# Loading an expert's gate, up and down weights as one transfer of 12 KB rows, and another order of the first attention output products

## The chip, the cores and the metric

The kernel runs on one core of one Trainium2 chip. The metric is the device time of one launch in microseconds (us), the median of several runs. The kernel before took 1279.79 us (three runs, 1278.62 to 1281.28).

## What is computed

One inference step of a one-layer streaming encoder, for 1024 prompt tokens, 128 sample tokens (8 streams of 16) and 16 meta tokens, width 1024, all in 32-bit floats. After an input projection, a pooling branch and a sparse attention (8 heads, 2 key and value heads), the two branches are merged, and a mixture of experts follows:

```
x1 = x + W_out( sig(g_A) * Pool(h) + sig(g_B) * (Attn(h) @ w_attn_out) ),   h = RMSNorm(x)
h2 = RMSNorm(x1);  each of 1152 tokens picks one group of 8 experts and 2 experts in it
out = x1 + sum over its 2 experts of  weight * ( silu(h2 @ w_gate[e]) * (h2 @ w_up[e]) ) @ w_down[e]
```

There are 32 experts. Gate and up are 1024 x 128 each and down is 128 x 1024: 512 KB each, 1.5 MB an expert. The last step is a final RMSNorm.

## The kernel before

Each engine runs its own program, written out by hand in `build`, and they meet at semaphores. SP issues nearly all plain transfers, on one queue, in program order; POOL issues the indirect ones (gathers and scatters) on another.

**Attention output** (PE from line 1198, evacuation by DVE from line 2086). For each of 8 columns of output features `c`, PE computes three products, one for each 384 tokens (`TOK3`), from the attention result in two parts (`o_hi`, `o_lo_p` or `o_lo_s`) and the weights in two parts (`wao_hi`, `wao_lo`). Product `u = 3c + j` goes to bank `u % 4`, and from `u = 4` PE waits for the evacuation of `u - 3` (`b6_evac`). DVE multiplies by the gate (`sB`, loaded by SP at line 807) and adds the pooling part. PE waits once, at line 1198, until all 24 attention groups have been written out by DVE (`a_oe`, lines 2028 and 2029). The groups run over blocks of 128 tokens from the last to the first, so the last group written is that of tokens 0 to 127. SP waits for the same at line 814, and then loads weights, gates, `w_out` (4 MB in rows of 4 KB, line 824) and x. ACT splits each column's weights (line 1650) and POOL forms their rest (line 2498).

**Output projection, routing** (PE from line 1284). Nine tiles of 128 tokens. SP stores the normalized rows to `h2_d` (line 866), and the first expert weights are loaded between those stores: experts 0 to 3 whole, the down weights of expert 6 early (line 864), experts 4 and 5, and gate and up of expert 6 last (line 872).

**Experts** (PE from line 1380). `list_d` holds each expert's tokens; an expert takes up to 128 rows. Weights live in seven slots (`eslot`, 12 KB in each of 128 partitions: gate, up, down). For expert `e` PE runs `gate_up_split(e)` (lines 1361, 1362, 1365), transposes the gathered rows of `e + 1` (line 1333), multiplies expert `e - 1`'s activations by its down weights (line 1346), and turns the activations (line 1371). ACT copies the high parts of gate and up of expert `e + 2` (`expert_upper`, lines 1786 and 1787), after waiting for all three pieces:

```
act.wait_ge(ew_in[e % NSLOT], 48 * (e // NSLOT + 1))
```

The gate and up product of `e` waits for these parts. ACT also scales half of the down product (line 1801), DVE the other half (line 2239). POOL then scatters the rows of expert `e - 1` to `y_d` (line 2525) and, in program order before the next scatter, issues the gather for expert `e + 3` into one of three buffers (line 2520). Gathers skip places past the end of a list, and so do scatters.

SP's loop at line 884 refills the slots: gate and up of `e + 7` as two transfers once `gate_up_split(e)` is done (`gu_done`, lines 842 and 843), the down weights of `e + 7` once expert `e`'s down product is done (`dn_done`, line 847), which comes after gate and up of `e + 8` in the queue. The three arrays `wg`, `wu` and `wd` lie apart in DRAM, and each transfer has 128 rows of 4 KB. An expert with more than 128 tokens is finished by a loop at line 2552, which loads weights into slot 0 again.

**End** (from line 895): SP loads the experts' rows back (line 900, two neighbouring rows at a time, 8 KB in one piece), PE and DVE add them, and the result is normalized and stored.

## Time and profile before

| | |
|---|---|
| median of 3 runs | 1279.79 us (1278.62 to 1281.28) |
| the profiled execution | 1279.34 us, its span in the profile 1277.5 us |
| PE busy | 1227.9 us, 96% of the span |
| PE weight loads | 1068.0 us, 84% |
| DVE, ACT, POOL busy | 917.7, 511.9 and 440.8 us |
| mean granted TensorE clock | 0.989 of full speed |
| moved by transfers | 163.84 MB in 79457 packets |
| chain that ended last | PE 84%, DMA 6%, POOL 3%, ACT 3%, DVE 2% |

The profile is one execution of the program. Times are from the start of the span. "PE" is TensorE, "PEld" its weight loads, "SPq" SP's queue of instructions. A name such as L847 is a line of the kernel. In a timeline, "x4" counts merged instructions, and brackets hold the idle time of the engine before the first of them and what ended it. "Share" in a table of stretches is the mean busy share of the core's 16 transfer engines.

### The profile page before, as it was taken

The page shows a single profiled execution, that of the slowest core. Times are in us where ns is not written, and L with a number is a line of the kernel's source. Part 1 is how long each engine was busy: PE and PEld are TensorE (multiplying, and loading weights), DVE is VectorE, ACT ScalarE, POOL GpSimd, SP SyncE. Part 2 cuts the span into 40 slices and gives each one's busy share as a digit, 9 for nine tenths or more (in the row PEclk, how much of TensorE's full clock was granted, in tenths as well). Part 3 has the DMA queues.
Part 4 walks back from the last instruction along what each step waited for, and adds up shares of the span by engine and source line. Part 5 has one row for each costly group of instructions (what it writes and reads, how often), then busy time and mean ns, then how long its engine had stood idle before and what let it go on. Part 6 is the DMA issues. An engine that isn't in the chain of part 4 may idle for free.

```text
span 1277.5 us, 21420 instructions
## 1 busy us (share of the span) xinstructions
PE 1227.9 (96%) x7577; PEld 1068.0 (84%) x7577; DVE 917.7 (72%) x2179; ACT 511.9 (40%) x1117; POOL 440.8 (35%) x740
## 2 busy tenths in 40 slices
PE   6999999999999999998999999999999979999987
PEld 6999999999999999998777766999788858887753
DVE  5667888889998999874677776232666668877747
ACT  6554323232321112224666554000432247766634
POOL 5803565676873115654000010210011233433310
PEclk9999999999999999998999999999999989999998
DMA  7201322222223221103000231944321469999749
GB/s 274 72 28 56 99 65 79 42 79 42 71 56 121 90 70 53 34 1 104 2 1 17 63 95 58 324 136 162 116 83 47 153 227 334 364 336 348 291 172 366
DMA packets 79457, 163.84 MB, mean 128 GB/s; under 512 B 12418, under 2 KB 48082, under 8 KB 78210
## 3 DMA queue, kind: packets, MB, share of 16 engines
q1 hardware_dynamic: 64977, 128.84, 29.6%
q0 software_dynamic: 12656, 27.62, 6.5%
q10 hardware_dynamic: 1728, 6.10, 1.2%
q8 instruction: 61, 1.00, 0.3%
q14 instruction: 35, 0.28, 0.1%
HBM read 137.86 MB, written 39.21 MB: 139 GB/s over the span
## 4 chain that ended last, share of the span: by engine, by line
PE 84%; DMA 6%; POOL 3%; ACT 3%; DVE 2%; SPq 1%; issue 1%; POOLq 0%; ACTq 0%; DVEq 0%
PE bank L921 12%; PE bank L920 12%; PE bank L922 12%; PE bank L1133 5%; PE bank L1115 3%; PE bank L1214 3%; PE bank L1208 3%; PE bank L1346 2%; PE bank L1051 2%; PE bank L1225 2%; PE bank L1226 2%; PE bank L1227 2%; DMA region_t<-ffn_input_scratch,small_i 2%; DMA region_h<-in_wd 2%; PE bank L1210 2%; PE bank L1361 1%
## 5 line engine op out<-in xcount | busy, mean ns | idle before, releaser
L1961 DVE MAX8 small<-region_kv 128x8 f32<-128x272 f32 (+4 forms) x241 | 190.2, 828 | 47.6 <-DVE region_kv L1966 47.5
L920 PE MATMUL bank<-h_hi,w_hi 128*128 128x384 f32 (+1 forms) x576 | 196.1, 340 | 0.0
L921 PE MATMUL bank<-h_lo,w_hi 128*128 128x384 f32 (+1 forms) x576 | 196.1, 340 | 0.0
L1966 DVE MATCH_REPLACE8 region_kv<-small,region_kv 128x272 f32<-128x272 f32 (+4 forms) x241 | 195.5, 818 | 0.0
L922 PE MATMUL bank<-h_hi,w_lo 128*128 128x384 f32 (+1 forms) x576 | 194.4, 338 | 0.0
L920 PE MATMUL bank<-w_hi,h_hi 128*128 128x256 f32 x448 | 128.8, 288 | 1.0 <-ACT region_q L1511 1.0
L2323 POOL TENSOR_TENSOR w_lo<-w_stage,w_hi 128x512 fp32r<-128x512 f32 x64 | 80.8, 1295 | 141.2 <-ACT w_hi L1450 141.1
L922 PE MATMUL bank<-w_hi,h_lo 128*128 128x256 f32 x448 | 125.9, 281 | 0.0
L921 PE MATMUL bank<-w_lo,h_hi 128*128 128x256 f32 x448 | 125.9, 281 | 0.0
L922 PEld LDWEIGHTS bank<-h_hi,w_lo 128*128 128x128 f32 x576 | 108.7, 189 | 0.0
L921 PEld LDWEIGHTS bank<-h_lo,w_hi 128*128 128x128 f32 x576 | 108.2, 188 | 0.6
L920 PEld LDWEIGHTS bank<-h_hi,w_hi 128*128 128x128 f32 x576 | 108.0, 187 | 0.5
L1609 ACT ACTIVATE region_q<-bank 128x384 f32<-128x384 f32 x48 | 23.6, 492 | 158.1 <-PE bank L922 158.1
L920 PEld LDWEIGHTS bank<-w_hi,h_hi 128*128 128x128 f32 x448 | 84.2, 188 | 1.7 <-ACT region_q L1511 1.2
L922 PEld LDWEIGHTS bank<-w_hi,h_lo 128*128 128x128 f32 x448 | 84.4, 188 | 0.0
L921 PEld LDWEIGHTS bank<-w_lo,h_hi 128*128 128x128 f32 x448 | 84.3, 188 | 0.0
L2525 POOL DMA_INDIRECT expert_rows_scratch<-region_t,small_i x32 | 39.0, 1218 | 109.8 <-ACT region_t L1801 87.8
L1133 PE MATMUL bank<-region_t,region_kv 128*128 128x512 f32 (+1 forms) x144 | 72.6, 594 | 0.1
L1214 PE MATMUL bank<-o_hi,wao_lo 128*128 128x384 f32 x192 | 67.9, 353 | 0.0
L1361 PE MATMUL bank<-expert_high,rowsT_hi 128*128 128x256 f32 x256 | 65.0, 292 | 1.5 <-ACT rowsT_hi L1794 1.5
L1208 PE MATMUL bank<-o_hi,wao_hi 128*128 128x384 f32 x192 | 64.9, 338 | 1.5 <-DVE o_lo_prompt L2029 1.5
L2094 DVE TENSOR_TENSOR region_t<-bank,region_t 128x384 f32<-128x384 f32 x24 | 13.4, 557 | 73.6 <-PE bank L1214 63.4
(350 smaller groups left out, 3066.5 us busy)
## 6 DMA issues: line engine op xcount, KB each, us to landing
w_stage<-in_w_in SPq DMA_DIRECT2D x72, 256.0 KB, 3.2
region_kv<-in_xa SPq DMA_DIRECT2D x16, 512.0 KB, 5.8
region_h<-in_wg SPq DMA_DIRECT2D x15, 512.0 KB, 5.2
region_h<-in_wu SPq DMA_DIRECT2D x15, 512.0 KB, 13.6
region_h<-in_wd SPq DMA_DIRECT2D x15, 512.0 KB, 19.3
region_q<-in_wd SPq DMA_DIRECT2D x12, 512.0 KB, 19.0
region_q<-in_wg SPq DMA_DIRECT2D x12, 512.0 KB, 6.0
region_q<-in_wu SPq DMA_DIRECT2D x12, 512.0 KB, 14.2
```

The source lines that it names most:

```text
L920: mm(out, st_hi(k), mv_hi(k), start=(k == 0), stop=False)
L921: mm(out, st_hi(k), mv_lo(k), start=False, stop=False)
L922: last = mm(out, st_lo(k), mv_hi(k), start=False, stop=(k == KD - 1))
L1115: last = nc.tensor.transpose(bank[3 + t % 2][0:rows, r * P:(r + 1) * P], probs_of(x, r)[:, k0:k0 + rows], ident)
L1133: mm(out[:, :], values[0:rows, :], PT[0:rows, t % 3, :], start=(j == 0), stop=False, skip_group_check=True)
L1208: mm(out, hi, o_hi[:, k, c0:c1], start=(k == 0), stop=False, skip_group_check=True)
L1214: last = mm(out, lo, o_hi[:, k, c0:c1], start=False, stop=(k == KD - 1), skip_group_check=True)
L1361: mm(out, rowsT_hi[:, par, k, :], high[:, :, k, :], start=(k == 0), stop=False, skip_group_check=True)
L1961: nc.vector.max(m8[:, q, :], x).then_inc(dve_c, 1)
L1966: nc.vector.match_replace(x, m8[:, q, :], x, TAKEN).then_inc(dve_c, 1)
L2323: tt(w_lo(n)[:, kk * m:kk * (m + 1), :], stage(s if s < KD else s % 4, kk, wd), w_hi(n)[:, kk * m:kk * (m + 1), :].bitcast(F32), ALU.subtr ...
L2525: pool.indirect_dma_start(out=y_d, out_offset=bass.IndirectOffsetOnAxis(ap=idx, axis=0), in_=src, in_offset=None, bounds_check=2 * TOK - 1 ...
```

## The change

- `wg`, `wu` and `wd` become one array `we`, in which partition row `p` of expert `e` holds gate, up and down one after the other, 12 KB.
- A slot is refilled by one transfer of 128 rows of 12 KB, issued when the down product of the slot's expert is done. SP's loop waits for `dn_done` alone.
- Expert 6 is still loaded in two parts, down early, gate and up late, now from rows of `we`. ACT's wait counts 16 instead of 48, and one more 16 for that slot.
- The loop for overfull lists loads one transfer instead of three.
- For output column `c = 0`, the three products run over tokens 384 to 767, 768 to 1151, then 0 to 383. PE waits for 23 of the 24 attention groups before the first and for all 24 before the third. DVE's evacuation follows the same order. The other columns are as before.

```diff
@@ -414,6 +414,7 @@
 
 
         COL3 = [(0, 400), (400, 784), (784, COLS)]
+        OUT3 = [[1, 2, 0]] + [[0, 1, 2]] * (KD - 1)
         TOK3 = [(0, 384), (384, 768), (768, 1152)]
 
         PIECES = [("idx", 0, C_IDX, IDXW), ("v", 0, C_KV + 256, 256), ("k", 0, C_KV, 256)]
@@ -837,18 +838,9 @@
             for t in range(7, NT):
                 load_x2(t)
 
-            def load_gate_up(e):
+            def load_e(e):
                 s = e % NSLOT
-                sp.dma_start(eslot[s][:, 0:1024], a["wg"][e]).then_inc(ew_in[s], 16)
-                sp.dma_start(eslot[s][:, 1024:2048], a["wu"][e]).then_inc(ew_in[s], 16)
-
-            def load_down(e):
-                s = e % NSLOT
-                sp.dma_start(e_down(s), a["wd"][e]).then_inc(ew_in[s], 16)
-
-            def load_e(e):
-                load_gate_up(e)
-                load_down(e)
+                sp.dma_start(eslot[s][:, :], a["we"][e]).then_inc(ew_in[s], 16)
 
             sp.wait_ge(b6_done, 24)
             for t in range(4, 7):
@@ -861,7 +853,8 @@
                 if t == 7:
                     sp.wait_ge(m_low, NT)
                     load_e(3)
-                    load_down(NSLOT - 1)
+                    s = NSLOT - 1
+                    sp.dma_start(e_down(s), a["we"][s, :, 2048:3072]).then_inc(ew_in[s], 16)
                 sp.wait_ge(h2_ready, t + 1)
                 sp.dma_start(h2_d[t * P:(t + 1) * P, :], h2[:, t % 2, :]).then_inc(h2_out[t % 2], 16)
             sp.wait_ge(o7_done, 2 * NT)
@@ -869,7 +862,8 @@
             sp.wait_ge(h2_last_out, 16)
             load_e(5)
             sp.wait_ge(hg_in[0], 16)
-            load_gate_up(NSLOT - 1)
+            s = NSLOT - 1
+            sp.dma_start(eslot[s][:, 0:2048], a["we"][s, :, 0:2048]).then_inc(ew_in[s], 16)
 
             def overflow_table_out():
                 sp.wait_ge(over_ready, 1)
@@ -881,13 +875,9 @@
                 sp.dma_start(over_row[0:1, 0:MAX_OVER], over_d.rearrange("n o -> o n")[:, 0:MAX_OVER]).then_inc(over_in, 16)
                 sp.dma_start(over_row[0:1, 31:32], over_d.rearrange("n o -> o n")[:, 31:32]).then_inc(over_in, 16)
 
-            for e in range(NE - NSLOT + 1):
-                if e < NE - NSLOT:
-                    sp.wait_ge(gu_done, e + 1)
-                    load_gate_up(e + NSLOT)
-                if e >= 1:
-                    sp.wait_ge(dn_done, e)
-                    load_down(e - 1 + NSLOT)
+            for e in range(NE - NSLOT):
+                sp.wait_ge(dn_done, e + 1)
+                load_e(e + NSLOT)
                 if e == 2:
                     overflow_table_out()
             overflow_table_in()
@@ -1195,11 +1185,14 @@
                         qk(S_STEP[st], 0, m)
 
 
-            pe.wait_ge(a_oe, NG_ALL)
+            pe.wait_ge(a_oe, NG_ALL - 1)
             for c in range(KD):
                 pe.wait_ge(wao_low, c + 1)
-                for j, (c0, c1) in enumerate(TOK3):
-                    u = 3 * c + j
+                for n, j in enumerate(OUT3[c]):
+                    c0, c1 = TOK3[j]
+                    u = 3 * c + n
+                    if u == 2:
+                        pe.wait_ge(a_oe, NG_ALL)
                     if u >= 4:
                         pe.wait_ge(b6_evac, u - 3)
                     out = bank[u % 4][:, 0:384]
@@ -1400,7 +1393,7 @@
                             last = nc.tensor.transpose(bank[4 + hf][:, j * P:(j + 1) * P], hg[:, 0, k * P:(k + 1) * P], ident)
                     last.then_inc(te_done, 1)
                     pe.wait_ge(te_evac, 2 * NE + 1 + it)
-                    pe.wait_ge(ov_w, 48 * it + 48)
+                    pe.wait_ge(ov_w, 16 * it + 16)
                     gate_up(0, 0, 0)
                     pe.wait_ge(act_ready, NE + 1 + it)
                     down(0, 0)
@@ -1780,7 +1773,7 @@
                 nc.scalar.activation(silu[:, par, :], bank[6 + par][:, 0:P], ACT.Silu).then_inc(silu_done, 1)
 
             def expert_upper(e):
-                act.wait_ge(ew_in[e % NSLOT], 48 * (e // NSLOT + 1))
+                act.wait_ge(ew_in[e % NSLOT], 16 * (e // NSLOT + 1 + (e % NSLOT == NSLOT - 1)))
                 if e >= 2:
                     act.wait_ge(gu_done, e - 1)
                 cp(e_high[e % 2][:, 0, :, :], e_gate(e % NSLOT)).then_inc(wao_high, 1)
@@ -2086,8 +2079,9 @@
             for c in range(KD):
                 dve.wait_ge(sbi_in[c % 2], 16 * (c // 2 + 1))
                 dve.wait_ge(mu_in[c % 2], 16 * (c // 2 + 1))
-                for j, (c0, c1) in enumerate(TOK3):
-                    u = 3 * c + j
+                for n, j in enumerate(OUT3[c]):
+                    c0, c1 = TOK3[j]
+                    u = 3 * c + n
                     dve.wait_ge(b6_done, u + 1)
                     if u >= 2:
                         dve.wait_ge(m_ready, u - 1)
@@ -2553,9 +2547,7 @@
                     code = pool.value_load(over_row[0:1, bass.ds(it, 1)], min_val=0, max_val=NE * OVER_J - 1)
                     ex = pool.snap(code % NE, min_val=0, max_val=NE - 1)
                     row = pool.snap((code // NE) * (P * NE - NE) + code + P * NE, min_val=0, max_val=NE * (TOK - P) + NE - 1)
-                    for o, src in ((0, a["wg"]), (1024, a["wu"])):
-                        pool.dma_start(eslot[0][:, o:o + 1024], src[bass.ds(ex, 1), :, :].rearrange("o p c -> p (o c)")).then_inc(ov_w, 16)
-                    pool.dma_start(e_down(0), a["wd"][bass.ds(ex, 1), :, :].rearrange("o p f -> p (o f)")).then_inc(ov_w, 16)
+                    pool.dma_start(eslot[0][:, :], a["we"][bass.ds(ex, 1), :, :].rearrange("o p c -> p (o c)")).then_inc(ov_w, 16)
                     pool.dma_start(heads_o[:, :], list_d[bass.ds(row, P, NE), :],
                                    allow_slow_non_contiguous=True).then_inc(ov_l, 16)
 
@@ -2626,9 +2618,9 @@
         "w_out": f["w_out"][0],
         "wrout": np.concatenate([f["w_router_group"][0], f["w_router_expert"][0]], axis=1),
         "rbias": np.broadcast_to(np.concatenate([f["b_router_group"][0], f["b_router_expert"][0]]), (P, NG + NE)),
-        "wg": f["w_expert_gate"][0].reshape(NE, KD, P, DE).transpose(0, 2, 1, 3).reshape(NE, P, D),
-        "wu": f["w_expert_up"][0].reshape(NE, KD, P, DE).transpose(0, 2, 1, 3).reshape(NE, P, D),
-        "wd": f["w_expert_down"][0],
+        "we": np.concatenate([f["w_expert_gate"][0].reshape(NE, KD, P, DE).transpose(0, 2, 1, 3).reshape(NE, P, D),
+                              f["w_expert_up"][0].reshape(NE, KD, P, DE).transpose(0, 2, 1, 3).reshape(NE, P, D),
+                              f["w_expert_down"][0]], axis=2),
         "ckT": f["cache_k"][0].transpose(0, 2, 3, 1),
         "cv": f["cache_v"][0].reshape(DEC_B, CACHE, KVH * HD),
         "kiC": f["cache_idx_k"][0].transpose(0, 2, 1).reshape(DEC_B // 2, 2 * ID, CACHE),
```

## Rows read from the trace of the kernel before

**Rows 1.** The page's 40 slices of 31.9 us: transfer engines' busy tenths, and GB/s.
```profile
DMA  7201322222223221103000231944321469999749
GB/s 274 72 28 56 99 65 79 42 79 42 71 56 121 90 70 53 34 1 104 2 1 17 63 95 58 324 136 162 116 83 47 153 227 334 364 336 348 291 172 366
```

**Rows 2.** PE timeline (start us, length us), lines 1333 and 1346.
```profile
...
1053.57 1.88 PE L1346 MATMUL bank<-region_w,region_t 128*128 128x512 f32 x4
...
1059.14 1.88 PE L1346 MATMUL bank<-region_h,region_t 128*128 128x512 f32 x4
...
1216.76 1.09 PE L1333 MATMUL bank<-consts,region_t 128*128 128x128 f32 x8 [0.44 <-DMA region_t<-ffn_input_scratch,small_i]
1217.69 1.88 PE L1346 MATMUL bank<-region_w,region_t 128*128 128x512 f32 x4
```

**Rows 3.** ACT timeline, line 1786; in brackets the idle time before and what ended it.
```profile
...
1139.81 1.05 ACT L1786 CAST expert_high<-region_q 128x1024 fp32r<-128x1024 f32 x1 [1.46 <-DMA region_q<-in_wd]
...
1215.15 1.05 ACT L1786 CAST expert_high<-region_h 128x1024 fp32r<-128x1024 f32 x1 [2.40 <-DMA region_h<-in_wd]
```

**Rows 4.** Line 847, windows 1060:1066 and 1122:1128: time from issue to landing.
```profile
L847 SPq DMA_DIRECT2D region_h<-in_wd x1: 328/328/328, 1061.1 to 1061.1; - x1
...
DMA to landing us min/median/max: 7.7/7.7/7.7
...
L847 SPq DMA_DIRECT2D region_q<-in_wd x1: 327/327/327, 1122.7 to 1122.7; - x1
...
DMA to landing us min/median/max: 24.3/24.3/24.3
```

**Rows 5.** Line 2520 (gathers), windows 1040:1050 and 1094:1100.
```profile
L2520 POOL DMA_INDIRECT region_t<-ffn_input_scratch,small_i x4: 1007/1022/1059, 1039.9 to 1049.7; - x4
...
DMA to landing us min/median/max: 5.0/5.3/5.8
...
L2520 POOL DMA_INDIRECT region_t<-ffn_input_scratch,small_i x2: 1002/1003/1004, 1093.5 to 1099.0; - x2
...
DMA to landing us min/median/max: 8.5/8.5/8.6
```

**Rows 6.** Timelines of POOL and PE: a gather's issue, and its first use.
```profile
1059.71 1.01 POOL L2520 DMA_INDIRECT region_t<-ffn_input_scratch,small_i  x1 [0.30 <-issue]
...
1069.74 1.09 PE L1333 MATMUL bank<-consts,region_t 128*128 128x128 f32 x8 [0.17 <-DMA region_t<-ffn_input_scratch,small_i]
```

**Rows 7.** Stretches: length, five engines' busy us, granted clock, transfer engines' share, GB/s.
```profile
1172.00:1182.00 10.00, 9.67 (x65) 7.69 (x63) 6.96 (x10) 7.50 (x14) 2.03 (x3) 1.00 0.95 351
...
1206.00:1212.00 6.00, 6.00 (x39) 4.69 (x38) 4.93 (x7) 4.39 (x10) 2.02 (x2) 1.00 0.57 219
1212.00:1218.00 6.00, 5.56 (x38) 4.47 (x37) 4.14 (x7) 3.60 (x8) 2.02 (x2) 1.00 0.50 190
```

**Rows 8.** Same view: the 4 MB load of line 824, and the loads of line 900.
```profile
804.00:816.00 12.00, 12.00 (x76) 12.00 (x74) 4.61 (x9) 0.00 (x0) 0.00 (x0) 1.00 1.03 409
1240.00:1256.00 16.00, 11.62 (x21) 4.67 (x20) 8.68 (x9) 3.78 (x10) 0.00 (x0) 0.79 1.01 425
```

**Rows 9.** SP timeline, lines 842 and 847: loads of expert 7's gate and down weights.
```profile
...
1048.09 0.33 SPq L842 DMA_DIRECT2D region_w<-in_wg  x1
...
1055.48 0.33 SPq L847 DMA_DIRECT2D region_w<-in_wd  x1
```

**Rows 10.** Timelines of PE, DVE and POOL around the first attention output products.
```profile
...
793.01 0.45 PE L1208 MATMUL bank<-o_hi,wao_hi 128*128 128x384 f32 x1 [1.51 <-DVE o_lo_prompt L2029]
...
792.26 0.69 DVE L2029 TENSOR_TENSOR o_lo_prompt<-bank,o_hi 128x512 fp32r<-128x512 f32 x1
...
803.09 0.56 DVE L2094 TENSOR_TENSOR region_t<-bank,region_t 128x384 f32<-128x384 f32 x1 [10.13 <-DMA region_t<-gate_b_scratch]
...
806.29 0.56 DVE L2094 TENSOR_TENSOR region_t<-bank,region_t 128x384 f32<-128x384 f32 x1 [0.99 <-PE bank L1214]
...
798.46 4.77 POOL L2498 TENSOR_TENSOR wao_lo<-region_kv,wao_hi 128x1024 fp32r<-128x1024 f32 x2 [32.37 <-ACT wao_hi L1650]
```


## The prediction

> **What bounds the kernel now.** I read the page's slices first: TensorE is busy nearly everywhere, and the transfer engines are full only in slices 33 to 36, the expert stage, where the changed loads are [rows 1]. The PE timeline gives that stage's pace. The down products of experts 0 and 1 start at 1053.57 and 1059.14, so an undisturbed expert takes 5.57 us; that of expert 28 starts at 1217.69, where 28 such steps would give 1209.5 [rows 2]. TensorE thus lost 8.2 us, nearly all after expert 16. The ACT timeline names the reason: ACT splits expert 18's weights at 1139.81 after waiting 1.46 us for "in_wd", and expert 30's at 1215.15, still waiting [rows 3]. Twelve experts in 75.34 us is 6.28 us each: the pace of the transfers, 0.71 us above TensorE's.
>
> Which queue is late? The weights' queue falls behind unseen: down weights issued at about 1061 (expert 8) land in 7.7 us, those at 1122.7 (expert 19) in 24.3 [rows 4]. Expert 8's land at 1068.8 and expert 19's at 1147.0, 7.1 us per expert, hidden by seven slots until expert 18. The gathers do not fall behind: 5.0 to 5.8 us before the scatters begin, 8.5 us amid them [rows 5]. But their spare is small. The gather issued at 1059.71 was needed at 1069.57 (TensorE waited 0.17 us, to 1069.74), a window of 9.9 us, so 8.5 leaves 1.4 [rows 6].
>
> Two more readings. When the loads run out, the share is 0.57 and 0.50 at 219 and 190 GB/s, against 0.95 at 351 earlier, while a gather still ends late at 1216.76 [rows 2, 7]. So about half of the 16 engines carry the remaining work. That fits the code: 2304 list entries over 32 experts is 72 of 128 rows, and the rows past a list's end move nothing, so I take the low half as the loaded one. There an expert costs 24 weight rows (3 transfers of 128 rows over 16 engines) and up to 16 rows of gather and scatter. Second, a 4 KB row: 409 GB/s over 16 engines is 0.160 us; an 8 KB row at 425 is 0.308 [rows 8]. Forty rows are 6.4 us, near the measured 6.28, since some lists are shorter.
>
> **The change, part by part.** *12 KB rows.* By the two rates a row costs 0.012 us plus 0.148 per 4 KB (estimate), so 12 KB cost 0.457. Per expert and engine, 8 of these are 3.65 us where 24 small ones are 3.84: 0.19 us saved, pace 6.09. No load of 12 KB rows is in the trace; the ends are no saving, and twice this one.
>
> *Issue later.* Gate and up of expert 7 went out at 1048.09, its down weights at 1055.48 [rows 9]; now all three leave together at 1055.5. No expert is split before all three pieces are in, and expert 8's weights had 13.9 us of spare (needed at 1138.35 - 10 x 5.57 = 1082.65, landed 1068.8), so the later issue itself costs nothing while loads land within some 21 us. Queued behind SP's one remaining wait are the next load and the overflow table's small transfers, which nobody needs before the last expert. SP issues one transfer for three (0.33 to 0.43 us each), all off the path. The early loads of slots 0 to 3 carry the same bytes at the same places, ahead of the h2 stores: nothing, or some tenths either way.
>
> *Turns.* This is where I choose. Alone a gather lands in 5.3 us, amid loads in 8.5 [rows 5]. Its 8 rows and the scatter's 8 just before it on each loaded engine are 16; the 3.2 us extra are 20 rows of 0.160. So the two queues seem to alternate, about one weight row to one other row. If turns stay one row each, a weight turn now lasts 0.457 instead of 0.160. An expert then needs 8 turns for weights but 16 for gather and scatter: the weights' queue always gets done, and the queue behind which work piles up becomes the gathers'. Work per expert is 6.09 against TensorE's 5.57; the 0.52 left over each time now delays gathers, whose 1.4 us are spent in three experts, not weights, whose seven slots hid it for eleven. From expert 3 until the last load leaves at expert 24, TensorE goes at 6.09: 21 x 0.52 = 10.9 us lost. After that nothing is late. Against 8.2 now: **+2.7 us**. The seven slots stay full and hide nothing. Ends of this term: at pace 6.28, 14.9 lost, +6.7; at pace 5.90, 6.9 lost, -1.3.
>
> The Trainium skill, "DMA: Bandwidth & Descriptors", section "Queues, rings and completion order", says an engine rotates among queues at packet granularity and finishes one packet before it switches. By that rule a longer packet would enlarge the weights' share, as here, against the change. The trace agrees for small rows. If instead shares went by bytes the term would be the -2.7 of the first rival.
>
> *Columns 1, 2, 0.* TensorE stands still for 1.51 us until 793.01, when DVE's remainder of the last group (792.26 + 0.69) is written [rows 10]. That group holds tokens 0 to 127, in column 0 alone, now third. Three products end at about 806.1 (DVE takes the third at 806.29), 4.4 us each, so it is needed 8.7 us after the start. The removed wait is worth **-1.5 us**. What could be late next: the second output column's low weights, needed from 806.1 and now from 804.6, are ready by 803.2 (two POOL subtractions from 798.46); the fifth product, at 810.5 and now 809.0, needs the first evacuation, which starts at 803.09 when gates land. Both are covered, the first by only 1.4 us; had it failed, at most that gain is lost. Ends: 0 and -1.5.
>
> Sum: +2.7 - 1.5 = +1.2 us on the profiled execution's 1279.34 (span 1277.5 and 1.8 around it). The median of the runs is 1279.79, 0.45 higher, so **1281.0**. Case A's own range, from both terms' ends, is 1277.0 to 1286.5.
>
> **Rivals.** *B, weights stay the late queue* (turns by bytes or time). Pace of weights 7.1 x 3.65/3.84 = 6.76; 13.9 us of spare at expert 8 then lasts 13.9/1.19 = 11.7 experts instead of 9.0; as the first wait came at 18 and not 17, now at 21. Ten and a half experts x 0.52 = 5.5 us lost, -2.7, with columns -4.2: **1275.6**. For it: the one-to-one fit above cannot tell rows from bytes, since both queues' rows have 4 KB. Against: an 8 KB row costs hardly more than its bytes, as if it were served in one go.
>
> *C, slower: a turn is a whole transfer.* A gather meeting two turns of eight 12 KB rows lands after 5.3 + 1.3 (scatter) + 2 x 3.65 = 13.9 us. Gather, transposes, down product, scatter and the next gather into the same buffer form a loop over three experts; outside the landing it has 16.7 - 9.9 = 6.8 us. So an expert takes (13.9 + 6.8)/3 = 6.9 us, 21 x 1.33 = 28 lost, +19.8, with columns +18.3: **1298.1**. It decides once a gather takes over 3 x 6.09 - 6.8 = 11.5 us; one such turn (10.3) does nothing. Against: loads come once per expert and mostly before the scatter, so two full turns are rare.
>
> *D, a 12 KB row is served as three of 4 KB.* Then neither pace nor turns change, only columns: 1279.79 - 1.5 = **1278.3**. For it: nothing here shows a row above 8 KB in bulk. Against: 8 KB rows already run 4% faster, so rows do count.
>
> **How the numbers follow.** A 0.50, B 0.27, C 0.10, D 0.13. A measurement can tell 0.2%, 2.6 us. A gives slower 0.19, same 0.25, faster 0.06; B faster 0.22, same 0.05; D same 0.10, faster 0.03; C slower. Together faster 0.31, same 0.40, slower 0.29. The range takes A and D whole and B down to 1.1 us below its value, 1274.5 to 1286.5, and leaves out C and B's far edge.
>
> **What would show it.** Right: weights land within some 7 to 9 us all through; ACT no longer waits for weights; TensorE waits for gathers from about expert 4, their landing at 10 to 12 us; down products 6.1 us apart up to expert 24, then 5.57; TensorE's 1.5 us at 793 gone, with the output projection starting 1.5 us earlier. Wrong: landings of weights that still grow to over 20 us (B or D, told apart by their pace, 6.1 or 6.3), gathers beyond 12 us with idle transfer engines (C), or ACT or DVE late on the second column.

## The result, and the profile after

The changed kernel took **1299.37 us** (median of 4 runs, 1295.15 to 1304.06) against 1280.53 for the kernel before (4 runs, 1278.62 to 1281.43): 1.0144 times, 95% interval [1.0126, 1.0163]. It is slower by some 18 us, where 1281.0 was forecast with a range up to 1286.5. The profiled execution took 1299.39 with a span of 1297.6, 20.1 more than before's. (The recorded expectations below call the scatters of the experts' rows scatter-adds; nothing is added in them.)

The page's slices, as in [rows 1], with TensorE's granted clock above them:

```profile
PEclk9999999999999999998999999999999899998998
DMA  7201422222223222003000325644023468888749
GB/s 273 70 26 57 115 45 78 41 79 57 73 63 109 69 88 66 1 1 103 1 17 2 93 78 189 224 154 183 33 93 130 154 241 307 325 325 305 263 147 373
DMA packets 70384, 163.84 MB, mean 126 GB/s; under 512 B 11409, under 2 KB 47073, under 8 KB 65041
```

Four slices of the expert stage, 34 to 37 counted from 1, now move 305 to 325 GB/s, where they moved 334 to 364. The row of packets is to be read beside before's:

```profile
DMA packets 79457, 163.84 MB, mean 128 GB/s; under 512 B 12418, under 2 KB 48082, under 8 KB 78210
```

Packets of 8 KB or more were 79457 - 78210 = 1247 and are 70384 - 65041 = 5343. The 4096 new ones are 32 experts times 128 rows (for 31 experts rows of 12 KB, for expert 6 the 8 KB of gate and up): each long row travels as one packet.

PE timeline of the expert stage, as in [rows 2]; line 1326 is the transposes of the gathered rows (before: 1333), line 1339 the down product (before: 1346):

```profile
1050.81 1.88 PE L1339 MATMUL bank<-region_w,region_t 128*128 128x512 f32 x4
...
1061.96 1.88 PE L1339 MATMUL bank<-region_h,region_t 128*128 128x512 f32 x4
...
1068.36 1.09 PE L1326 MATMUL bank<-consts,region_t 128*128 128x128 f32 x8 [1.55 <-DMA region_t<-ffn_input_scratch,small_i]
1069.29 1.88 PE L1339 MATMUL bank<-region_h,region_t 128*128 128x512 f32 x4
...
1176.56 1.88 PE L1339 MATMUL bank<-region_q,region_t 128*128 128x512 f32 x4
...
1184.75 1.97 PE L1326 MATMUL bank<-consts,region_t 128*128 128x128 f32 x8 [3.34 <-DMA region_t<-ffn_input_scratch,small_i]
1186.51 3.62 PE L1339 MATMUL bank<-region_q,region_t 128*128 128x512 f32 x4
...
1243.74 1.88 PE L1339 MATMUL bank<-region_h,region_t 128*128 128x512 f32 x4
```

The stage starts 2.8 us earlier than before (1050.81 against 1053.57), of which some tenths are chance between executions, as the run with the columns alone will show. The first three down products keep TensorE's own pace of 5.57 us; the gather for the transposes at 1068.36, expert 5's, is the first that comes late. Expert 29's down product starts at 1243.74, 192.9 us after expert 0's, where 29 steps of 5.57 would be 161.5: TensorE lost 31 us in the stage. It lost them in 23 steps, from the down product of expert 2 (1061.96) to that of expert 25 (1221.51), 6.94 us each. Before it lost 8 up to expert 28. The pair at 1184.75 and 1186.51 shows a second thing: after a wait of 3.34 us the same eight transposes take 1.97 us instead of 1.09, and the same four products 3.62 us instead of 1.88.

The waits of that stretch (1045 to 1250 us: who waited for whom, us in total, times, longest) after:

```profile
POOL expert_rows_scratch L2519 <- ACT region_t L1794: 112.7, 28, 8.4
...
PE bank L1326 <- DMA region_t<-ffn_input_scratch,small_i: 20.4, 16, 3.3
```

and before, with the lines that no longer appear after:

```profile
ACT expert_high L1786 <- DMA region_q<-in_wd: 14.1, 6, 3.1
...
ACT expert_high L1786 <- DMA region_h<-in_wd: 11.2, 5, 2.5
...
ACT expert_high L1786 <- DMA region_w<-in_wd: 4.0, 2, 2.4
...
PE bank L1333 <- DMA region_t<-ffn_input_scratch,small_i: 3.1, 5, 1.7
```

ScalarE waited 29.3 us for weights before and waits for none now; TensorE's waits for gathers grew from 3.1 to 20.4 us. (The line of the scatters is GpSimd waiting for rows to send; it stood first before too, with 87.8 us.) The late queue has changed sides. The landings say the same. Line 843 is the one load of an expert, from 1055 to 1235 us; line 2514 is the gathers, from 1055 to 1090 and from 1090 to 1140. They stand beside [rows 4, 5]:

```profile
L843 SPq DMA_DIRECT2D region_w<-in_we x3: 328/328/328, 1099.3 to 1195.9; - x3
...
DMA to landing us min/median/max: 9.6/10.0/10.3
...
L2514 POOL DMA_INDIRECT region_t<-ffn_input_scratch,small_i x5: 1002/1005/1014, 1056.9 to 1085.2; - x5
...
DMA to landing us min/median/max: 11.2/12.7/14.1
...
L2514 POOL DMA_INDIRECT region_t<-ffn_input_scratch,small_i x8: 1002/1004/1005, 1090.9 to 1136.3; - x8
...
DMA to landing us min/median/max: 12.4/12.5/12.5
```

The view has a landing for few transfers only: three of the 24 loads, those into region_w, at 10.3, 10.0 and 9.6 us (before: 7.7 growing to 24.3), and two gathers in each stretch. A second reading agrees with it. A gather that TensorE waits for lands when the wait ends, and from their issue to that moment the 16 late gathers took 10.5 to 14.1 us, half of them 12.5 or less. Before, gathers from 1090 to 1140 us landed in 8.7.

Stretches as in [rows 7] (length, busy time of PE, PEld, DVE, ACT, POOL, granted clock, transfer engines' share, GB/s):

```profile
1140.00:1150.00 10.00, 8.76 (x60) 7.12 (x59) 6.62 (x10) 5.17 (x11) 4.59 (x4) 1.00 0.94 380
1160.00:1170.00 10.00, 8.04 (x44) 6.23 (x44) 5.30 (x7) 4.20 (x7) 3.24 (x3) 0.83 0.77 294
1180.00:1190.00 10.00, 6.66 (x26) 4.29 (x25) 3.17 (x5) 3.38 (x6) 2.49 (x2) 0.68 0.73 286
```

The granted clock is full in the first and 0.83 and 0.68 in the others, that is, for a third of the second stretch and almost two thirds of the third it was 1.2 instead of 2.4 GHz. Cut into eight stretches of 20 us from 1060 to 1220, the view reads 1.00 in all eight before, and now 0.95, 0.97, 1.00, 1.00, 1.00, 0.91, 0.83 and 0.91; twice what is missing to 1.00, times 20 us, is the time at the lower level, 17 us together. In the first stretch, at full clock, the transfer engines' share is 0.94.

One reading more, the view of the transfer queues from 1060 to 1180 us (packets, MB, the time that the packets took as a share of 16 engines), before:

```profile
q1 hardware_dynamic: 8274, 30.05, 68.5%
q0 software_dynamic: 5841, 11.78, 25.8%
```

and after:

```profile
q1 hardware_dynamic: 2596, 28.13, 63.8%
q0 software_dynamic: 5047, 10.16, 23.5%
```

The hardware queue is the weights', the software queue that of gathers and scatters. Sixteen engines have 1920 us there. Before, 30.05 MB took 68.5% of it, 1315 us, 22.8 GB/s per busy engine; after, 28.13 MB took 1225 us, 23.0 GB/s. In this stretch the long rows saved under 1% of the weights' transfer time, where 5% was forecast.

Last, the columns. The output product's first matmul, as in [rows 10]:

```profile
790.65 0.60 PE L1119 MATMUL bank<-nbuf,region_kv 128*128 128x256 f32 x2
790.89 0.52 PE L1201 MATMUL bank<-o_hi,wao_hi 128*128 128x384 f32 x1
```

It starts without a wait; the 1.51 us are gone.

### The profile page after: what moved, and what is told of

It is laid out like the page before. It is cut to its first block, busy times and chain, and to the rows that moved or that the text cites. A ratio compares the mean times of both kernels' runs of the same rounds, so it can differ in the third digit from the quotient of the medians.

```text
span 1297.6 us, 21357 instructions
## 1 busy us (share of the span) xinstructions
PE 1234.1 (95%) x7577; PEld 1071.2 (83%) x7577; DVE 921.5 (71%) x2179; ACT 513.9 (40%) x1117; POOL 449.2 (35%) x740
## 2 busy tenths in 40 slices
DMA packets 70384, 163.84 MB, mean 126 GB/s; under 512 B 11409, under 2 KB 47073, under 8 KB 65041
## 4 chain that ended last, share of the span: by engine, by line
PE 80%; DMA 9%; POOL 3%; ACT 3%; issue 2%; DVE 2%; SPq 0%; POOLq 0%; ACTq 0%; DVEq 0%
PE bank L911 12%; PE bank L910 12%; PE bank L912 12%; DMA region_t<-ffn_input_scratch,small_i 7%; PE bank L1123 5%; PE bank L1105 3%; PE bank L1207 3%; PE bank L1201 3%; PE bank L1041 2%; PE bank L1218 2%; PE bank L1219 2%; PE bank L1220 2%; PE bank L1339 2%; PE bank L1203 2%; PE bank L1084 1%
## 5 line engine op out<-in xcount | busy, mean ns | idle before, releaser
L2519 POOL DMA_INDIRECT expert_rows_scratch<-region_t,small_i x32 | 47.5, 1483 | 124.5 <-ACT region_t L1794 116.4
L2226 DVE TENSOR_TENSOR rowsT_lo<-bank,rowsT_hi 128x512 fp32r<-128x512 f32 x64 | 41.4, 687 | 41.1 <-ACT rowsT_hi L1787 39.1
```

Of the source, the lines that this page charges most:

```text
L2226: tt(rowsT_lo[:, e % 2, ks, :], bank[4 + hf][:, :].rearrange("p (k t) -> p k t", k=4), rowsT_hi[:, e % 2, ks, :].bitcast(F32), ALU.subtrac ...
L2519: pool.indirect_dma_start(out=y_d, out_offset=bass.IndirectOffsetOnAxis(ap=idx, axis=0), in_=src, in_offset=None, bounds_check=2 * TOK - 1 ...
```

## The experiments

My theory after this reading: the change moved lateness from the weights' queue, with seven slots of reserve, to the gathers' queue, with 1.4 us of reserve, and it is the *length of the rows*, not the moment or the number of transfers, that slows the gathers. Each run is compared with runs of the kernel before from its own session, whose medians were 1280.8 to 1281.9. Rivals: the later issue of gate and up; the one large transfer, which goes ahead of gathers as a whole; the layout in DRAM; the columns.

### Columns alone

Before, with the columns in the order 1, 2, 0 and nothing else.

```diff
-            pe.wait_ge(a_oe, NG_ALL)
+            pe.wait_ge(a_oe, NG_ALL - 1)
...
-                for j, (c0, c1) in enumerate(TOK3):
-                    u = 3 * c + j
+                for n, j in enumerate(OUT3[c]):
+                    c0, c1 = TOK3[j]
+                    u = 3 * c + n
+                    if u == 2:
+                        pe.wait_ge(a_oe, NG_ALL)
...
```

> The kernel before with the output columns in the order 1, 2, 0 and nothing else; weights as before. Every theory of the expert stage: 1.5 to 2.8 us faster than before (0.1% to 0.2%): the changed kernel's stage began 2.8 us earlier (down product of expert 0 at 1050.81, before 1053.57), of which the removed wait is 1.5. Expert pace as before: 164 us from the down product of expert 0 to that of expert 28.

Measured: 1278.38 us (12 runs), 0.9983 of before [0.9974, 0.9992], -2.2 us. The columns are a gain, a little above the 1.5 forecast, and no part of the slowdown. The stage of this execution began only 0.3 us before that of the kernel before (first down product at 1053.29 against 1053.57), but this execution was already 2.1 us late ahead of the columns. Counted from the last matmul before the output products (793.05 here, 790.91 before), the first down product comes after 260.24 us instead of 262.66: 2.4 us earlier. In the changed kernel it is 260.16 us. So the columns make 2.5 of its 2.8 us. They give more than the wait of 1.51; where the rest comes from was not traced.

### The later issue alone

Before, with all three transfers of an expert issued behind its slot's down product, rows still 4 KB.

```diff
-            for e in range(NE - NSLOT + 1):
-                if e < NE - NSLOT:
-                    sp.wait_ge(gu_done, e + 1)
-                    load_gate_up(e + NSLOT)
-                if e >= 1:
-                    sp.wait_ge(dn_done, e)
-                    load_down(e - 1 + NSLOT)
+            for e in range(NE - NSLOT):
+                sp.wait_ge(dn_done, e + 1)
+                load_e(e + NSLOT)
```

> The kernel before (three arrays, three transfers of 4 KB rows an expert), but all three issued after the down product. Theory T, turns: what makes gathers late is the length of a weight row, 12 KB against 4; then this kernel keeps gathers at 8.5 to 9 us and is within 4 us of before (landings of weights still grow past 20 us). Theory M, moment: what hurts is that 1.5 MB leave at once, just before scatter and gather; then it loses 15 to 23 us like the changed kernel, with gathers landing after 11 us.

Measured: 1285.89 us (6 runs), 1.0037 [1.0023, 1.005], +4.7 us, just beyond the 4 us that the theory of turns allowed. ScalarE's waits for weights rose from 29.3 to 40.8 us, TensorE's for gathers from 3.1 to 4.1. The forecast had priced this part at nothing; it costs about 5 us when the rows stay short, and the weights are still the late queue there. That they are later because they start later is my reading of it; no run took it apart.

### One transfer, short rows

The changed kernel, columns included, but each expert as one transfer of 384 rows of 4 KB from three places in DRAM.

```diff
-                sp.dma_start(eslot[s][:, :], a["we"][e]).then_inc(ew_in[s], 16)
+                sp.dma_start(eslot[s].rearrange("p (o c) -> p o c", o=3), a["we"][e].rearrange("o p c -> p o c")).then_inc(ew_in[s], 16)
...
-        "we": np.concatenate([f["w_expert_gate"][0] ...
+        "we": np.stack([f["w_expert_gate"][0] ...
```

> The changed kernel whole (columns too, one transfer an expert, at the end of the down product), but gate, up and down lie in three blocks of DRAM rows, so that the one transfer has 384 rows of 4 KB. Theory T: gathers at 8.5 to 9 us, time between 4 us under and 3 us over before, thus some 17 to 22 us under the changed kernel. Theory M, or a theory that one big transfer is the unit of a turn: as the changed kernel, 15 to 22 us over before.

Measured: 1286.11 us (5 runs), 1.0038 [1.0024, 1.0053], some 2 us above the range of the theory of turns, with gathers a little later than its 8.5 to 9 us. The kernel with three late transfers had no columns in it; with their 2.2 us taken off it would stand at 1283.7, so the joining of three transfers into one may cost some 2 us (the next experiment is its direct partner). The gathers from 1090 to 1140 us:

```profile
DMA to landing us min/median/max: 8.6/10.2/10.9
```

Against the changed kernel this one is 13.3 us faster, and only the rows' length and their place in DRAM differ. So rival C's cause, a turn that lasts a whole transfer, is out: here the transfer is as large as in the changed kernel.

### The same layout, short pieces

The changed kernel with its array in DRAM and its moment of issue, the 12 KB fetched as three transfers of 4 KB pieces.

```diff
-                sp.dma_start(eslot[s][:, :], a["we"][e]).then_inc(ew_in[s], 16)
+                for o in range(0, 3072, 1024):
+                    sp.dma_start(eslot[s][:, o:o + 1024], a["we"][e, :, o:o + 1024]).then_inc(ew_in[s], 16)
...
```

> The changed kernel with its layout in DRAM and its moment of issue, but the row of 12 KB fetched as three transfers of 4 KB pieces. Theory (it is the length of the row that one descriptor moves, not where the bytes lie in DRAM): as with one transfer of 4 KB rows from separate places, 1284 to 1288 us, gathers 8.6 to 10.2 us, loads of the weights late for ScalarE; some 13 us under the changed kernel. Rival (the layout with three matrices side by side costs by itself, rows of neighbouring partitions being 12 KB apart): it stays at 1295 to 1300.

Measured: 1283.65 us (10 runs), 1.0021 [1.0011, 1.0031], a little under the range given, 15.7 us under the changed kernel and 2.5 under the one transfer of short rows, though the two intervals overlap a little: the joining costs some 2 us or nothing. ScalarE waits for weights again, TensorE's waits for gathers fall from 20.4 to 5.0 us. The layout by itself costs nothing.

### Half-long rows at the old moment

Before, with gate and up joined in one transfer of 8 KB rows, issued when they were before; down weights apart.

```diff
-                sp.dma_start(eslot[s][:, 0:1024], a["wg"][e]).then_inc(ew_in[s], 16)
-                sp.dma_start(eslot[s][:, 1024:2048], a["wu"][e]).then_inc(ew_in[s], 16)
+                sp.dma_start(eslot[s][:, 0:2048], a["wgu"][e]).then_inc(ew_in[s], 16)
...
```

> The kernel before, but gate and up lie in one row of DRAM and come by one transfer of 8 KB rows, at the old moment (gate and up product done); down as before with 4 KB rows. Theory T: 16 weight turns an expert of 0.23 us on average instead of 24 of 0.16; scatter and gather need 16 turns too, so both queues get late together: gathers at 9 to 11 us, 2 to 10 us slower than before. Theory M: same moment as before, so within 1 us of it, gathers at 8.5.

Measured: 1298.46 us (4 runs), 1.0139 [1.0123, 1.0154], +17.7 us: as slow as the whole change, where 2 to 10 us were expected. TensorE's waits for gathers from 1045 to 1250 us, and the gathers from 1090 to 1140:

```profile
PE bank L1332 <- DMA region_t<-ffn_input_scratch,small_i: 21.2, 22, 2.0
```

```profile
L2519 POOL DMA_INDIRECT region_t<-ffn_input_scratch,small_i x8: 1006/1007/1007, 1090.5 to 1137.0; - x8
...
DMA to landing us min/median/max: 12.4/12.8/13.9
```

The gathers land as late as with 12 KB rows (the 22 that TensorE waited for took 10.6 to 14.0 us from their issue to the end of the wait, median 12.9), and no wait for weights is left. So the slowdown needs neither the later issue nor rows of 12 KB. Its granted clock is 1.00 through the loop, and the loop is 194.2 us long from the first down product to the last, against 200.0 in the changed kernel, whose waits for gathers are about as long in all (20.4) but longer one by one (up to 3.3 against 2.0). That 8 KB rows slow a gather as much as 12 KB rows do was not forecast by any theory here, and stays unexplained.

### The other side: rows of 2 KB

Before, with every expert load cut into rows of 2 KB.

```diff
-                sp.dma_start(eslot[s][:, 0:1024], a["wg"][e]).then_inc(ew_in[s], 16)
+                sp.dma_start(halves(eslot[s][:, 0:1024]), a["wg"][e].rearrange("o p c -> p o c")).then_inc(ew_in[s], 16)
...
```

> The kernel before with every expert load cut into rows of 2 KB, still three transfers at their old moments: only the row length changes, to the other side. Theory (the two queues take turns row by row on a loaded engine, so the time a gather needs amid loads grows with the weight row): gathers land faster than before in the stretch 1090 to 1140 us, 7 to 7.5 us against 8.5, no wait of TensorE for them at all, while the weights get a smaller share of the loaded engines and more overhead per row, so that ScalarE waits for weights more than before's and the kernel is 1 to 6 us slower (1282 to 1287). Rival (the queues take turns by bytes or by whole transfer): gathers land as before, 8.5 us within 0.3, and only the row overhead shows.

Measured: 1286.24 us (4 runs), 1.0048 [1.0029, 1.0066], +5.4 us. From 1045 to 1250 us:

```profile
ACT expert_high L1789 <- DMA region_h<-in_wd: 17.7, 7, 3.2
ACT expert_high L1789 <- DMA region_q<-in_wd: 15.3, 6, 2.6
...
ACT expert_high L1789 <- DMA region_w<-in_wd: 5.3, 2, 2.7
...
PE bank L1336 <- DMA region_t<-ffn_input_scratch,small_i: 0.2, 1, 0.2
```

TensorE's waits for gathers go from 3.1 to 0.2 us, ScalarE's for weights from 29.3 to 38.3. With rows of 2, 4, 8 and 12 KB, TensorE waits 0.2, 3.1, 21.2 and 20.4 us for gathers. From 2 to 8 KB that is what turns taken row by row would give; that 12 KB adds nothing to 8 KB is not. The kernel is slower all the same, since the late weights now set a pace of 6.5 us (13 steps of the down product from 1138.31 to 1222.76 us), where it was 6.28 with rows of 4 KB. The trace of this kernel gives no landing times for its gathers, so the 7 to 7.5 us expected for them stay untested.

### Lists spread over all transfer engines

The forecast took it that rows past a list's end move nothing, and that the low half of the places, and so half of the 16 engines, carries all gathers and scatters. The test is a constant: the r-th entry of a list gets place `place`, so that entries fall on all engines evenly. Nothing else changes.

```diff
-    c[:, K_END:K_END + P] = np.arange(P)
+    r = np.arange(P)
+    g = r % 16
+    place = np.zeros(P, np.float32)
+    place[64 * (g // 8) + 4 * (g % 8) + (r // 16) % 4 + 32 * (r // 64)] = r
+    c[:, K_END:K_END + P] = place
```

For the kernel before:

> The kernel before, but place r of an expert's list stands on another partition, so that the filled places (72 of 128 on average) lie over all 16 transfer engines instead of half of them; only a constant changes. If half of the engines carried gathers and scatters, each now has 24 weight rows and 9 others, 33 x 0.16 = 5.3 us an expert, under TensorE's 5.57: ACT stops waiting for weights, gathers land in 7 us or less, and the 8 us lost in the stage come back: 6.5 to 9 us faster. If the load was even before, no change.

Measured: 1270.78 us (6 runs), 0.9927 [0.9908, 0.9946], some 10 us faster, a little more than expected. Two of its stretches:

```profile
1100.00:1120.00 20.00, 20.00 (x138) 16.73 (x137) 16.81 (x22) 14.01 (x25) 7.66 (x8) 1.00 1.02 395
...
1200.00:1220.00 20.00, 20.00 (x136) 16.53 (x135) 15.07 (x20) 12.56 (x23) 6.55 (x6) 1.00 0.24 81
```

The engines are full at 395 GB/s, TensorE is busy without a gap, and the loads end early instead of at the end. No wait for weights or gathers is left in the loop. The Trainium skill, "DMA: Bandwidth & Descriptors", section "The descriptor swizzle", gives the assignment by which `place` was made: in a transfer of 128 partitions, 0 to 63 belong to engines 0 to 7, in fours of neighbours, two fours to each engine, and the others to engines 8 to 15. The run agrees with it in that the share rises to 1.02; no view here shows a single engine.

For the changed kernel:

> The changed kernel with the same spread lists. Turns theory: only 9 turns with 12 KB weight rows stand before a gather's end instead of 16, and work per engine is 5.1 us an expert; gathers land in under 9.5 us and are never waited for: 1269 to 1274 us, 25 to 30 under the changed kernel, slightly better than the 4 KB kernel with spread lists. If the turn were a whole transfer (8 rows of 12 KB, whatever the gather's size), gathers would stay near 12 us and the time over 1290.

Measured: 1277.09 us (10 runs), 0.9966 [0.9953, 0.9979], -22.3 against the changed kernel, 3 us short of the range. TensorE still waits 3.9 us for gathers, 6 times, and the loop has no piece at half clock.

### The gather ahead of the scatter

GpSimd issues the gather of expert e+3, then the scatter of e-1. Here the scatter is put one expert later in GpSimd's program, so that the gather of e+3 is issued before the scatter of e-2 and no longer behind it.

```diff
-            for e in range(NE + 1):
+            for e in range(NE + 2):
...
-                if e >= 1:
-                    y = e - 1
+                if e >= 2:
+                    y = e - 2
```

In the changed kernel:

> The changed kernel, but POOL issues the gather for expert e + 3 before the scatter of expert e - 2 instead of after it, some 4.4 us earlier. If late gathers are the whole loss, their window grows from 9.9 to 14.3 us, over the 12.5 they take: pace in the stage at most the transfers' work (6.1 to 6.3 us), only after some ten experts, time 1274 to 1284 us. If something else costs (clock, weights, ACT), it stays over 1290.

Measured: 1291.64 us (4 runs), 1.0087 [1.0063, 1.011], far above the 1274 to 1284 expected if the gathers' window were the whole loss. TensorE's waits for gathers fall to 16.4 us only, and a new one appears, from 1045 to 1250 us:

```profile
DVE region_t L2233 <- DMA expert_rows_scratch<-region_t,small_i: 24.5, 14, 2.6
PEld bank L1326 <- DMA region_t<-ffn_input_scratch,small_i: 20.0, 17, 4.7
PE bank L1326 <- DMA region_t<-ffn_input_scratch,small_i: 16.4, 15, 4.5
ACT region_t L1794 <- DMA expert_rows_scratch<-region_t,small_i: 8.4, 11, 1.4
```

VectorE and ScalarE now wait for a scatter to free its buffer. The window did grow, and the gathers took it up: the 15 that TensorE waited for landed 15.7 to 20.2 us after their issue, with a median of 17.5, instead of 12.5. The lateness also went from one user of the queue to the other: the whole queue is late, not one wait in it. From 1147.22 to 1212.54 us ten experts take 6.53 us each.

In the kernel before:

> The kernel before with the gather ahead of the scatter. Its gathers are hardly waited for, and its weights are the late queue, so within 1.5 us of before; ACT still waits for weights from about expert 18.

Measured: 1281.71 us (10 runs), 1.0004 [0.9991, 1.0017]. Nothing, as the late queue there is the weights', and no wait for a scatter appears either.

### A fourth buffer for gathers

What set the pace of 6.5 us, where 6.09 was forecast? The pace is that of the changed kernel at full clock: ten experts from 1090.38 to 1156.12 us take 6.57 us each. The loop over three buffers, (12.5 + 6.8)/3 = 6.4, gives about that; so would 6.5 us of plain work on the loaded engines. A fourth buffer lengthens the loop and leaves every transfer as it is.

```diff
+        NHG = 4
+        hgb = [hg[:, i, :] for i in range(3)] + [RW[:, 5120:6144]]
...
-                if e + 3 < NE:
+                if e + NHG < NE:
                     pool.wait_ge(te_done, 2 * (e + 1))
-                    gather(hg[:, e % 3, :], gidx[:, e + 3:e + 4], hg_in[e % 3])
+                    gather(hgb[e % NHG], gidx[:, e + NHG:e + NHG + 1], hg_in[e % NHG])
...
```

> The changed kernel with a fourth buffer for gathered rows, in 4 KB per partition of region_w that nothing uses in this stage: the gather of expert e+4 leaves when expert e is transposed. Every transfer stays as it is, rows and bytes; only the loop gather, transposes, next gather into the buffer spreads over four experts. Loop theory (an expert takes (landing + 6.8)/3 because a gather has 9.9 us and lands in 12.5): (12.5 + 6.8)/4 = 4.8 us, under TensorE's 5.57, so TensorE's waits for gathers fall from 20.4 us to under 5, with them most half-clock stretches, and the time to 1276 to 1284, unless scatter-adds, which still have three buffers, become late in their place (waits of VectorE for them, up to 1290). Work theory (the loaded transfer engines need about 6.5 us for an expert's rows, 12 KB rows being slower amid the stage than alone): the pace stays 6.3 to 6.6 us once the extra buffer is spent, gathers land 5 us later than now, 16 to 18 us, and the time is 1293 to 1300.

Measured: 1292.67 us (4 runs), 1.008 [1.0056, 1.0103], 6.7 under the changed kernel. Its gathers from 1140 to 1200 us, and two of its down products, six experts apart at full clock:

```profile
L2516 POOL DMA_INDIRECT region_t<-ffn_input_scratch,small_i x6: 1005/1006/1009, 1148.7 to 1187.9; - x6
...
DMA to landing us min/median/max: 15.1/18.2/19.5
```

```profile
1181.82 1.88 PE L1341 MATMUL bank<-region_q,region_t 128*128 128x512 f32 x4
...
1220.80 1.88 PE L1341 MATMUL bank<-region_q,region_t 128*128 128x512 f32 x4
```

A gather takes 5.7 us longer than with three buffers, and the pace is (1220.80 - 1181.82)/6 = 6.50 us. The twelve gathers of the whole stage that TensorE waited for took 15.9 to 19.3 us, median 18.2. A transfer that takes longer by just what it was given is waiting in a queue: the pace comes from the queue, not from the number of buffers for gathers. The first late gather is expert 9's instead of expert 5's; then the extra buffer was spent. The time is at the edge of what the work theory gave and 9 us above the loop theory's range. One reservation: the scatters kept three buffers, and VectorE waited 20.4 us for them, so a part of theirs in the 6.50 is not excluded. Against a large one: with the engines evenly loaded, the same three buffers keep TensorE's pace with rows of 12 KB (below). The run also still has some 10 us at half clock (0.89, 0.94 and 0.91 in three of the eight stretches from 1060 to 1220 us).

In the kernel before:

> The kernel before with the same fourth buffer. It separates what the buffer gives by itself: before waits for gathers 3.1 us in all, and its pace of 6.3 us after expert 18 is the weights' lateness. Both theories: waits for gathers gone, waits of ScalarE for weights 29 to 33 us in all, time 1278 to 1281. If it gained more than 3 us, the gathers would have been a part of the old bound that the reading of the profile before missed.

Measured: 1281.31 us (10 runs), 1.0 [0.9988, 1.0011]. Without the long rows the buffer is worth nothing.

### The best of both

Before, with spread lists and the columns:

> The kernel before with the two parts that gained by themselves: the list places spread over all transfer engines (0.9927 of before) and the columns in the order 1, 2, 0 (0.9983). Theory (the stage is paced by the gather loop, whose length is set by how long a few loaded engines keep the gathers; the columns act only ahead of the stage): the two gains lie in different stages and add up, 0.9927 x 0.9983 = 0.991 of before, about 1269.3 us (1268 to 1270.5), first down product near 1051.5 and an expert every 5.6 us. Rival (an earlier start of the stage is given back by a later landing somewhere in it): the stage is 2 us longer than with the lists alone and the time stays at 1270.8 to 1272.

Measured: 1269.85 us (6 runs), 0.9918 [0.9904, 0.9933], as expected: the two gains add up.

The changed kernel (12 KB rows, one transfer, columns) with spread lists and the gather ahead of the scatter:

> The changed kernel with both remedies for late gathers: list places spread over all transfer engines, and the gather of expert e+3 issued ahead of the scatter-add of e-2. With spread places alone it took 1277.1 us and still had 3.9 us of waits for gathers, 6 times. Theory (rows of 12 KB cost time only because gathers and scatter-adds wait longer behind them; the weights themselves are never late in this form): without the scatter-add ahead of the gather no gather is late, and it runs 1270 to 1274 us, the rest being scatter-adds that free their buffers late (waits of VectorE on the scatter-adds of up to 3 us in all). Rival (the order only moves the lateness from gathers to scatter-adds one for one): it stays at 1276 to 1278, with 4 us or more of waits for scatter-adds.

Measured: 1268.66 us (6 runs), 0.9907 [0.9892, 0.9922], a little under the range. No wait for gathers, weights or scatters is left in its expert loop. The queues from 1060 to 1180 us, first with 4 KB rows (spread lists and columns):

```profile
q1 hardware_dynamic: 9283, 33.69, 74.0%
```

and with 12 KB rows:

```profile
q1 hardware_dynamic: 3109, 33.56, 71.0%
```

That is 23.7 against 24.6 GB/s per busy engine: with even load the long rows do save 4%, near the 5% that the forecast counted on. But TensorE sets the pace of both kernels, so it buys nothing that can be told: their intervals overlap. Both beat the kernel before by 10 to 12 us.

## Why the prediction was wrong

**What held.** TensorE's 5.57 us, the late weights' queue and the gathers' 1.4 us of reserve were read rightly. What case A said would happen did happen: the weights always get done and the work piles up behind the gathers, because of the rows' length. Weights land in about 10 us (7 to 9 were named), ScalarE waits for none, TensorE first waits ahead of expert 3's down product, and from expert 25's on the pace is 5.57 us again. The rule of the Trainium skill that spoke against the change ("DMA: Bandwidth & Descriptors", section "Queues, rings and completion order": queues alternate by packet) is the one that the runs with rows of 2, 4 and 8 KB bear out in its direction; the step from 8 to 12 KB it does not explain. That uneven load was the bound is shown by the spread lists. B falls, since the weights are never late; D falls by the packet count and by the time.

**The step that failed** is the term "turns": "TensorE goes at 6.09: 21 x 0.52 = 10.9 us lost". In its place the trace has 23 steps of 6.94 us, 31.4 us lost. The side on which the lateness fell was right, its size was not, for three reasons of unequal certainty.

1. *The pace.* 6.09 was 6.28 less 0.19 for the shorter service of long rows, and even the worst end was 6.28. At full clock the changed kernel shows 6.57, and the fourth buffer's run 6.50. The 0.19 was taken from transfers that had the engines to themselves, 0.160 and 0.457 us a row. Amid the stage 4 KB went at 22.8 GB/s and 12 KB at 23.0, about 0.18 and 0.53 us: no saving. At 6.50 the loss is 21 x 0.93 = 19.5 us, +11.3 against the 8.2 of before instead of +2.7; over the 23 steps that were slow it is 21.4. Why it is 6.50 and not 6.28 is open: the views don't separate the 16 engines, so whether the loaded ones were slower per row or stood empty in between can't be read from them.
2. *Gathers that land at 12.5 us have no reserve at all.* The forecast let them land at 10 to 12 and took the spare as spent once. Where the late thing had seven slots, a slow transfer was smoothed by the next; with three buffers each one is a wait of TensorE. With 8 KB rows the whole loop took 194.2 us where it takes 168.7 undisturbed (first to last down product with spread lists and columns), 25.5 us lost over 22 experts, 1.2 each, a pace of 6.7 without any half clock. How much of the changed kernel's loss beyond the pace of 6.50 is this and how much the next was not taken apart: the fourth buffer's 6.7 us have a share of both.
3. *The clock.* Waits of 2 to 3.3 us for gathers were followed by 17 us at half clock, worth up to 8.5 us. The forecast had no term for it. The changed kernel's runs rank the same way: mean granted clocks of 0.988, 0.986, 0.982 and 0.981 with 1295.15, 1299.34, 1299.39 and 1304.06 us. With 8 KB rows there is none of it and the loop is 5.8 us shorter at the same sum of waits. One wait there was 1.99 us long and no fall followed, where one of 1.97 in the changed kernel was followed by a fall, so the length of a wait alone does not tell when the clock falls.

**Rival C** gave 1298.1, nearly the measured time, by (13.9 + 6.8)/3 = 6.9 us. Its threshold (gathers above 11.5 us decide) fits the runs: landings of 8.5 to 10.9 us go with a few us of loss, those about 12.5 with 18. Its cause was wrong: one transfer of short rows, of the same size, costs 13.3 us less. That its price fits is luck: it put the landing at 13.9 us, with the measured 12.5 its own formula gives 6.4 and not 6.9, and the measured 6.94 contain the half clock, for which it had no term. And the loop of three experts is how the late queue reaches TensorE, not what makes it slow, as the fourth buffer indicates.

**Issue later** was forecast at nothing. With short rows it costs 4.7 us; with long rows nothing shows, as 8 KB rows at the old moment are as slow as the whole change. The parts, in this order, add up: columns -2.2, late issue +4.7 (sum 2.5, measured 2.7 by the ratio of the short pieces), one transfer +2.5 (hardly beyond the intervals), long rows +13.3, in all +18.3. But they are not independent, since 8 KB rows on top of the old moment are +17.7 by themselves.

**Columns** were forecast at -1.5 and gave -2.2, interval -1.0 to -3.3, so the size held; by the traces it is 2.4 us (above).

## What to carry to other kernels

Where two queues share the transfer engines, lengthening one's rows can slow the other (gathers from 8.7 to 12.5 us here); ask which of them has reserve before giving the other the longer turn. A queue that falls behind in silence behind seven slots is the cheaper one to be late. And look at how evenly the small irregular transfers load the engines first: here one constant was worth four times the columns' gain, and with the order of gather and scatter changed as well the row length no longer mattered (with the constant alone the changed kernel still took 1277.09 us against 1270.78).

## What the runs showed beyond that

- Waits of TensorE for gathers do not grow evenly with the row: 0.2, 3.1, 21.2 and 20.4 us at 2, 4, 8 and 12 KB, gathers landing in 8.7, 12.8 and 12.5 us (median of the few with a landing, 1090 to 1140 us) at the last three.
- The uneven load of the engines cost some 10 us in a stage where the page shows them 9 tenths busy on average. The share read 0.92 to 0.98 over 20 us stretches; with even lists it reads 0.99 to 1.02 until the loads run out, and 359 to 396 GB/s instead of 337 to 373.
- A wait of 3.34 us in a loop that otherwise runs at full clock was followed by a fall to the lower clock, with 1.97 instead of 1.09 us for the same transposes.
- In the Trainium skill, "DMA: Bandwidth & Descriptors", section "Rules for kernel authors", the advice for bandwidth is transfers of 1 MiB and more, and many small ones are to be joined. Here 512 KB transfers joined into 1.5 MB ones of unchanged rows gave 1286.11 against 1283.65 us: no gain, perhaps a loss. The 13.3 us more that the long rows cost are no test of that advice, which speaks of a transfer's size.
